# Last two output tiles of a diffusion trunk in parts of 384 and 128 tokens, the scale of the 128 by one product with ones

## The reference, cut to what matters

```python
def rmsnorm(x, g):
    xf = x.astype(jnp.float32)
    y = xf * lax.rsqrt(jnp.mean(xf * xf, axis=-1, keepdims=True) + EPS) * g.astype(jnp.float32)
    return y.astype(x.dtype)
...
    return (o * jax.nn.silu(z)) @ w_out          # ret_output
...
        x = x + gt_l[:, None, :] * ol
...
    return rmsnorm(x, final_g)
```

## Time and profile before

| | us |
|---|---|
| median of 3 runs | 953.13 |
| lowest and highest | 952.37, 954.92 |
| the profiled execution | 953.86 |
| its span, first to last instruction | 952.1 |
| TensorE busy in the span | 929.2 |
| VectorE, ScalarE, GpSimd busy | 556.5, 346.2, 243.7 |

### The profile page before, as it was taken

How to read it: one execution, slowest core, us unless ns; L and a number is a source line. 1 busy time by engine, 2 the same in 40 slices (tenths; PEclk the granted TensorE clock), 3 DMA queues, 4 the chain that set the end, 5 groups by cost and what they waited for, 6 DMA issues and landing times.

```text
span 952.1 us, 13121 instructions
## 1 busy us (share of the span) xinstructions
PE 929.2 (98%) x4852; PEld 804.2 (84%) x4852; DVE 556.5 (58%) x817; ACT 346.2 (36%) x587; POOL 243.7 (26%) x243
## 2 busy tenths in 40 slices
PE   5999999999999999999999999999999999999996
PEld 5989998888888888888888888888888888888886
DVE  6887769999985332358435545436435545468333
ACT  8443334323223332345323333324223333454222
POOL 4359840766554000014100321013100221011001
PEclk9999999999999999999999999999999999999998
DMA  9762233655545121212221122202211122102222
GB/s 353 290 222 86 92 111 112 202 180 193 185 168 225 64 67 67 89 45 89 67 67 45 45 70 86 66 1 88 66 66 44 44 66 66 56 10 89 92 85 88
DMA packets 28859, 98.71 MB, mean 104 GB/s; under 512 B 3816, under 2 KB 6024, under 8 KB 28560
## 3 DMA queue, kind: packets, MB, share of 16 engines
q1 hardware_dynamic: 26800, 91.04, 28.2%
q0 software_dynamic: 1744, 6.84, 1.9%
q10 hardware_dynamic: 272, 0.26, 0.1%
HBM read 96.01 MB, written 2.10 MB: 103 GB/s over the span
## 4 chain that ended last, share of the span: by engine, by line
PE 90%; DVE 4%; issue 2%; DMA 2%; POOL 1%; ACT 1%; SPq 0%; POOLq 0%; DVEq 0%
PE banks L1681 30%; PE banks L1682 29%; PE banks L1683 29%; DMA raw<-stream 1%; DVE wreg L1162 1%; DVE hreg L1431 0%; POOL gate L640 0%; DMA gate<-x_rows 0%; DVE gate L1153 0%; DVE gate L1156 0%; DVE hreg L1208 0%; PE banks L1952 0%; DVE dist L1172 0%; POOL gate L680 0%; PE banks L1825 0%
## 5 line engine op out<-in xcount | busy, mean ns | idle before, releaser
L1681 PE MATMUL banks<-hreg,ring 128*128 128x512 f32 (+2 forms) x940 | 334.0, 355 | 3.8 <-DVE hreg L1208 2.3
L1682 PE MATMUL banks<-hreg,ring 128*128 128x512 f32 (+2 forms) x940 | 332.1, 353 | 0.0
L1683 PE MATMUL banks<-hreg,ring 128*128 128x512 f32 (+2 forms) x940 | 330.0, 351 | 0.0
L1072 DVE TENSOR_TENSOR ring<-raw,ring 128x512 fp32r<-128x512 f32 x192 | 148.7, 790 | 231.8 <-ACT ring L692 230.5
L692 ACT ACTIVATE ring<-raw 128x512 fp32r<-128x512 f32 x192 | 118.9, 630 | 363.6 <-PE banks L1683 285.5
L1681 PEld LDWEIGHTS banks<-hreg,ring 128*128 128x128 f32 x940 | 177.8, 189 | 29.4 <-issue 3.6
L1683 PEld LDWEIGHTS banks<-hreg,ring 128*128 128x128 f32 x940 | 177.4, 189 | 22.2
L1682 PEld LDWEIGHTS banks<-hreg,ring 128*128 128x128 f32 x940 | 177.8, 189 | 21.7 <-issue 1.0
L607 POOL TENSOR_TENSOR gate<-xreg,gate 128x257 f32<-128x257 f32 (+1 forms) x64 | 72.3, 1160 | 75.5 <-ACT gate L834 58.0
L1104 DVE CUSTOM_DVE_ANT_0 dist<-raw,gate 128x1024 bf16<-128x1024 f32 x64 | 84.9, 1327 | 4.1 <-DMA raw<-stream 0.5
L640 POOL TENSOR_TENSOR gate<-gate 128x512 f32<-128x512 f32 x12 | 17.2, 1430 | 250.7 <-ACT gate L915 249.9
(11 more groups left out here) (224 smaller groups left out, 1099.6 us busy)
## 6 DMA issues: line engine op xcount, KB each, us to landing
raw<-stream SPq DMA_DIRECT2D x148, 512.0 KB, 3.3
gate<-stream SPq DMA_DIRECT2D x10, 512.0 KB, 11.0
gate<-x_rows SPq DMA_DIRECT2D x6, 512.0 KB, 6.9
gate<-x_lat POOLq DMA_DIRECT2D x1, 2048.0 KB, 8.7
xreg<-x_lat POOLq DMA_DIRECT2D x1, 2048.0 KB, 9.0
xreg<-stream SPq DMA_DIRECT2D x2, 512.0 KB, 12.5
gate<-cond_in SPq DMA_DIRECT2D x2, 512.0 KB, 9.1
gate<-x_ctx POOLq DMA_DIRECT2D x1, 1024.0 KB, 11.5
```

Source lines behind the costliest of these rows:

```text
L1072: dve.tensor_tensor(ring[:, n % 2, 1, c], raw[:, buf, c], f32(ring[:, n % 2, 0, c]), ALU.subtract).then_inc(split_done, 1)
L1681: pe.matmul(out, left[0], right[0], start=start, stop=False)
L1682: pe.matmul(out, left[0], right[1], start=False, stop=False)
L1683: return pe.matmul(out, left[1], right[0], start=False, stop=stop)
```

## The change

Tiles 6 and 7 are both made in two parts, the first of 384 tokens (`first`) and the second of 128 (`rest`), in the order: tile 6 first, tile 7 first, tile 7 rest, tile 6 rest. Since tile 6's weights are then used at the start and at the end, they are split into a place of their own, `w6` in `wreg` (columns 4096 to 8191), which is free by then; tile 7's weights go to `ring`. The loops over tiles 2 to 5 are written out on ScalarE and VectorE.

For the first 384 tokens the scale is made as before (three columns instead of two, one bank instead of two), inside the matmuls of the two `rest` parts: `sums_first` after kk 8 of tile 7 rest, `rows_first` after kk 1 of tile 6 rest. For the last 128 tokens the squares are the moving operand and the matrix of ones the weights (bank 5): this gives every partition the sum of each token at once. `sums_rest` adds acc_t and tile 7's squares after kk 10 of tile 6 rest; only tile 6's squares come after the last projection matmul. Square root and reciprocal then run on 128 columns, and no diagonal matrix and no second product are needed.

ScalarE multiplies all eight tiles by the final gain into tmp_t (`gain`), tiles 0 to 5 ahead of the parts. VectorE writes all outputs in instructions over two or four tiles (`scale_out`); GpSimd has no part in it any more. The stores are four of 2 tiles by 384 tokens and two of 4 tiles by 128 tokens, all on SyncE's queue.

```diff
@@ sync
+            first, rest = slice(0, FIRST), slice(FIRST, LAT)
+            for n, (c, a, b) in enumerate([(first, 2 * i, 2 * i + 2) for i in range(4)] +
+                                          [(rest, 4 * i, 4 * i + 4) for i in range(2)]):
+                sp.wait_ge(out_vec, n + 1)
+                sp.dma_start(out[a:b].rearrange("m p t -> p m t")[:, :, c],
+                             x3[:, a:b, c]).then_inc(s_out, 16)
@@ scalar
+            for n in (HOME1, HOME1 + 1):
+                buf, landed = raw_at("out1", n)
+                act.wait_ge(s_raw[buf], landed)
...
+                    act.activation(w6[0][:, n - HOME1, c], raw[:, buf, c], ACT.Copy).then_inc(hi_done, 1)
+            x2_sq(5, 1)
...
+            for m in range(6):
+                gain(m, slice(0, LAT))
...
+            def part_sq(n, m, c):
+                act.wait_ge(x2_part_done, n)
+                act.wait_ge(acc_done, m + (2 * KT + 4))
+                act.activation(sq_t[:, m % 2, c], x3[:, m, c], ACT.Square).then_inc(sq_part, 1)
+                gain(m, c)
+
+            part_sq(1, 6, first)
+            part_sq(2, 7, first)
+            act.wait_ge(sum_sq_done, 3)
+            act.activation(tok_rms[:, 0:3], bank(0, 3), ACT.Sqrt, scale=1.0 / D,
+                           bias=eps[:, :]).then_inc(end_root, 1)
+            part_sq(3, 7, rest)
+            part_sq(4, 6, rest)
+            act.wait_ge(sum_sq_done, 4)
+            act.activation(rstd_t[:, rest], bank(5, P), ACT.Sqrt, scale=1.0 / D,
+                           bias=eps[:, :]).then_inc(end_root, 1)
@@ vector
+            def scale_out(a, b, c, rstd):
+
+                n = b - a
+                dve.tensor_tensor(x3[:, a:b, c], tmp_t[:, a:b, c],
+                                  rstd.unsqueeze(1).to_broadcast([P, n, c.stop - c.start]),
+                                  ALU.mult).then_inc(out_vec, 1)
...
+            x2_part(3, 7, rest, bank(4, P))
+            dve.wait_ge(rows_spread, 1)
+            dve.wait_ge(gained, 6)
+            dve.wait_ge(x2_part_done, 2)
+            for m in (0, 2, 4):
+                scale_out(m, m + 2, first, bank(1, FIRST))
+            dve.wait_ge(gained, 8)
+            scale_out(6, 8, first, bank(1, FIRST))
+            x2_part(4, 6, rest, bank(3, P))
+            dve.wait_ge(end_root, 2)
+            link(dve.reciprocal(rstd_t[:, rest], rstd_t[:, rest]))
+            dve.wait_ge(gained, 10)
+            for m in (0, 4):
+                scale_out(m, m + 4, rest, rstd_t[:, rest])
@@ tensor
+            def last_part(m, c, o, between):
+
                 for kk in range(FT):
+                    if c is first and kk % 4 == 0:
+                        split(SLOT_OUT1 + 2 * m + kk // 8, kk // 4 % 2)
+                    if m == 6:
+                        w = tuple(w6[part][:, kk // 8, P * (kk % 8):P * (kk % 8) + P] for part in range(2))
+                    else:
+                        w = part_of(kk // 8, P * (kk % 8))
+                    last = mm3(o, w, (g1(kk, 0)[:, c], g1(kk, 1)[:, c]), kk == 0, kk == FT - 1)
+                    if kk in between:
+                        between[kk]()
+                last.then_inc(end_part, 1)
+
+            pe.wait_ge(x1_done, 6 + (2 * KT + 3))
+            last_part(6, first, bank(7, FIRST), {})
+            pe.wait_ge(x1_done, 7 + (2 * KT + 3))
+            last_part(7, first, bank(6, FIRST), {})
+            last_part(7, rest, bank(4, P), {8: sums_first})
+            last_part(6, rest, bank(3, P), {1: rows_first, 10: sums_rest})
+            pe.wait_ge(sq_part, 4)
+            pe.matmul(bank(5, P), ones[:, :], sq_t[:, 0, rest], start=False,
+                      stop=True).then_inc(sum_sq_done, 1)
```

More of the change, by code:

```diff
@@ L1670, in _, with x2_part @@
-            dve.wait_ge(x2_half, 2)
-            for m in (6, 7):
-                last_out(0, m)
-            token_rstd(1)
-            for m in range(POOL_TILES[1], KT):
-                last_out(1, m)
+            first, rest = slice(0, FIRST), slice(FIRST, LAT)
+            def x2_part(n, m, c, src):
+                dve.wait_ge(end_part, n)
+                dve.scalar_tensor_tensor(out=x3[:, m, c], in0=src, scalar=mod1[:, 24 + m, 0:1],
+                                         in1=x3[:, m, c], op0=ALU.mult,
+                                         op1=ALU.add).then_inc(x2_part_done, 1)
@@ L2070, in _ @@
-            pe.wait_ge(x2_half, 1)
-            for part in (acc_t, squares7):
-                if part is squares7:
-                    pe.wait_ge(sq_half, 2)
-                for b, i in ((6, 2), (7, 3)):
-                    last = pe.matmul(bank(b, 1), part[:, P * i:P * i + P], ones[:, 0:1],
-                                     start=part is acc_t, stop=part is squares7)
-            last.then_inc(sum_sq_done, 1)
-            token_rows(1)
+            for m in (4, 5):
+                pe.wait_ge(x1_done, m + (2 * KT + 3))
+                out_tile(SLOT_OUT1 + 2 * m, ((0, LAT, bank(7 - m % 2)),), g1)
@@ new lines, in _, with sums_first, rows_first @@
+            first, rest = slice(0, FIRST), slice(FIRST, LAT)
+            def sums_first():
+                pe.wait_ge(acc_part, 1)
+                pe.wait_ge(sq_part, 2)
+                for i in range(3):
+                    last = token_sum(bank(0, 1, i), i, (acc_t, sq_t[:, 1, :]))
+                last.then_inc(sum_sq_done, 1)
+            def rows_first():
+                pe.wait_ge(spread_done, 1)
+                for t in range(3):
+                    last = pe.matmul(bank(1)[:, P * t:P * t + P], ones[:, :], spread[:, t, :],
+                                     start=True, stop=True)
+                last.then_inc(rows_spread, 1)
@@ new lines, in sums_rest @@
+            def sums_rest():
+                pe.wait_ge(acc_done, 6 + (2 * KT + 5))
+                pe.matmul(bank(5, P), ones[:, :], acc_t[:, rest], start=True, stop=False)
+                pe.wait_ge(sq_part, 3)
+                pe.matmul(bank(5, P), ones[:, :], sq_t[:, 1, rest], start=False, stop=False)
+            def last_part(m, c, o, between):
+                for kk in range(FT):
+                    if c is first and kk % 4 == 0:
[8 more added lines that the diff above has]
+                last.then_inc(end_part, 1)
```

167 lines of the change are left out of this document (48 added, 119 removed).

## The result

| | us |
|---|---|
| kernel before, median of 5 runs | 953.13 (952.37 to 954.92) |
| changed kernel, median of 5 runs | 964.57 (962.11 to 964.79) |
| ratio, with its 95% interval | 1.011 (1.010 to 1.0121) |
| profiled execution of the changed kernel, its span | 962.11, 960.3 |

The change makes the kernel 1.1% slower, and 964.57 us lies outside the range that was forecast, 954.4 to 959.6.

The account below looks back on a forecast made before the run. TensorE, holding 90% of the chain of waits, was taken to bound the kernel. TensorE's +6.26 us and the tail's -3.65 us gave +2.6 us on 953.13, so 955.7 us, range 954.4 to 959.6.

Parts of the forecast that it names:

- TensorE's terms: TensorE up to its last projection matmul: 16.70 + 10.80 + 2.48 = 29.98 us against 23.72, 6.26 us later.
- The rival of overlapping weight loads: 128-column matmuls run at 0.081 us or 0.067 us each, giving 952.7 or 951.3 us, not slower; chance 0.06.
- the row: Profile row of 130-column matmuls, each with its own weight load: 0.113 us each; basis for 0.1125 us per 128-column matmul.
- The tail's terms: Chain behind the last projection matmul, residual to stores and end: 6.98 us against 10.63, 3.65 us saved.
- The store: Last store of 256 KB at the kernel's end: lands 2.5 us after issue, ends 2.3 and 3.4.
- The covers: Weight splits, ScalarE gains and VectorE's early outputs stay hidden behind TensorE; VectorE done 1.5 us before the last residual.
- The step that failed: In the 128-column parts the clock was taken to stay at full level; its fall was a rival, chance 0.2.
- the short stretch of 130 columns: Earlier stretch of 130-column matmuls at full clock, used as evidence against the clock falling in the 128-column parts.
- main case: All paces as the profile rows show: centre 955.7 us, from 954.8 to 957.0; chance 0.74.
- the long fall: All of tile 6 rest at half clock: 54 instructions x 0.11, 5.9 us more, 961.6 us; chance 0.08.
- that rival: The clock falls in the 128-column parts: 1.7 us more (957.4) or 5.9 us more (961.6); chance 0.2.

Follow-up runs that it names:

- e2: The changed kernel, with the six sums of the first 384 tokens streaming 128 columns of ones instead of one; 955.57 us, ratio 1.0036 to the kernel before.
- e6: The changed kernel, with the 128-token parts streaming 192 columns and using 128; 956.23 us, ratio 1.0034 to the kernel before.
- e9: The changed kernel, with VectorE adding tile 7's squares first, so 6 one-column instructions replace 12; 954.06 us, ratio 1.0017 to the kernel before.
- e1: The changed kernel, with the 128-token parts streaming 256 columns and using 128; 956.49 us, ratio 1.0048 to the kernel before.
- e4: The changed kernel, in the order tile 6 first, tile 6 rest, tile 7 first, tile 7 rest; 958.46 us, ratio 1.0064 to the kernel before.
- e5: The changed kernel measured again, unaltered; 962.7 us, ratio 1.0111 to the kernel before.
- e7: The kernel before, with the scale of tile 7's second half made by products with the matrix of ones; 954.0 us, ratio 1.0009.
- e10: Against the kernel before: tile 7 alone in 384 and 128 tokens (128 streamed as 192), GpSimd writing three output instructions; 954.34 us, ratio 1.001.

## Why the prediction was wrong

**TensorE's terms held as long as the clock did.** Both 384-column parts took 16.66 us (917.18 to 933.84; forecast 16.70). The 128-column pace was 0.1115 us and the 12 sums took 1.31 us to the next matmul (forecast 12 x 0.1125 = 1.35). The whole list, undisturbed, is e2's and e6's: 29.68 and 29.70 us against 23.60, so 6.1 us more where 6.26 was forecast.

**The rival of overlapping weight loads did not come.** Only the first matmul of a part followed after 0.06 us, as in the earlier trace rows; all others after 0.11. The Trainium skill, TensorE: Matmul & The Clock Gate, section Back-to-back issue gap, gives about 81 ns for such a stream; no stretch of matmuls of the last tiles shows it in any run here, and the row was the better guide.

**The tail's terms held too.** With the clock up, 7.30 us lie behind the start of the last matmul in e6, where before had 10.75: 3.45 us saved, forecast 3.65. The store landed after 2.5 us as taken. The covers held: VectorE was free 1.57 us before the last residual in e6, where 1.5 was forecast (6.16 in the slowed change), and TensorE did not stop.

Together, +2.65 us in e2 and e6 against the +2.6 forecast. That this is so close is in part luck: each of the two terms came out 0.2 us smaller, and the two errors cancel. Their ratios, 1.0036 and 1.0034, are some 0.7 us above that.

**The step that failed is the clock.** The argument "matmuls follow one another without a wait, and the short stretch of 130 columns kept 1.00" carried a main case of 0.74, and the long fall was left out of the range with a chance of 0.08. In the trace the matmuls do follow one another without a wait, TensorE is busy for 3.00 of every 3.00 us, and the clock falls. The price was sized about right: 54 instructions by 0.11, 5.9 us, 961.6; it was 56 instructions by 0.101 plus 0.44 in the tail, 6.1 us, and 962.11 for the profiled execution. (Tile 6 rest has 58 instructions, not 54: four of `sums_rest` were left out of the count.) The median, 964.57, is 2.5 us above that; see what stays open. Its chance was what was wrong.

What had been a clause in that rival, "in the middle the sums stream one column at a time", is one of two conditions. Taking away the one-column streaming (e2) or half of it (e9), or filling the 128-column matmuls to 192 or 256 (e6, e1), each keeps the clock at 1.00. Together with the 5.31 us of e4 without a fall: neither the thin matmuls nor the one-column products are enough alone, in this kernel at this place. The rows that the argument used were one with 8 thin matmuls and one with 12 short instructions among matmuls of 256 columns; neither has both, and I read them as if they spoke of the sum.

The trace of before had stronger evidence of both kinds, which the prediction left aside when it said that no stretch has such thin streaming for so long:

```profile
22.72 5.52 PE L1734 MATMUL banks<-csf,gate 128*128 128x128 f32 x48
24.00:28.00 4.00, 4.00 (x39) 4.00 (x38) 3.19 (x4) 1.13 (x1) 0.00 (x0) 1.00 1.03 416
411.35 1.89 PE L1916 MATMUL banks<-ones,gate 128*128 128x1 f32 x16
411.00:414.00 3.00, 3.00 (x28) 3.00 (x27) 0.40 (x2) 1.51 (x4) 0.00 (x0) 1.00 0.02 5
```

From 19.04 to 28.00 us TensorE issues 80 matmuls of 128 columns without a wait, and at 411.35 it issues 16 one-column instructions in a row between matmuls of 256 columns. The clock is at 1.00 in both. So each condition alone had been harmless at a size near the change's (96 thin matmuls, 12 one-column instructions), and the two together were seen nowhere.

The Trainium skill, same page, section HAM oscillation, blames waits between bursts for the falls of a thin-M kernel. By waits alone the packed stream would keep its clock; the measurement decides against it, since the stretch from 917.20 to the fall has no wait. It was used as an argument to lower the chance, and it should not have been.

**What stays open.** Three of the five runs of the change and one of the four of e5 took 2.2 to 2.8 us more than the others, with a mean granted clock of 0.985 or 0.986 instead of 0.987 to 0.989. They are part of why the change costs 10.5 us by the ratio and 8.8 by the traced stage. An estimate from the clock: 0.003 of 960 us is 2.9 us, so 5.8 us more at half level; that is 27 instructions at 0.2135 us, which cost 27 by 0.101, 2.7 us. That fits a fall 3 us earlier, at about 937.6, among the one-column sums. But no such execution was traced, and a low stretch elsewhere is not ruled out: in before, too, runs of 951.5 us have 0.997 and runs of 953.5 us 0.994, and what its trace has is half level from 56.6 to 60.0.

That low stretch shows another fall than this one: it began after TensorE had been idle for 2.25 us, behind eight matmuls of 130 columns, and the clock came back at 60.0 after 3.4 us of packed matmuls of 386 columns. Whether it would have come back near the end as well, had the matmuls grown dense again, isn't shown: in every fall of the last stage it stayed low to the end. And the runs show that both conditions together brought the fall, not why.

## What to carry to other kernels

Before cutting matmuls thinner to shorten a tail, look at what each stretch streams, and treat short products placed among thin matmuls as a risk to the clock even when TensorE never waits; the price is the number of instructions still to come times the difference between 0.2135 and 0.1125 us. Beside weight loads of 128 columns, up to 192 streamed columns were free here and can be streamed and thrown away to keep the clock. And where evidence about a cliff covers each of two conditions apart, the case that joins them belongs into the range.

## What the runs showed of the hardware that was not expected

- The granted clock fell from 1.00 to 0.50 with TensorE busy without a gap for more than 20 us (917.20 to 940.6), 2.5 us after 1.3 us of one-column matmuls inside a stretch of 128-column ones.
- At 0.50 the start-to-start time of a 128-column matmul with its own weight load went from 0.1115 to 0.2135 us, and the recorded weight load from 0.19 to 0.33 us. At full clock the columns do not set this pace (192 start as often as 128), and that was no shelter from the half level.
- Matmuls of 128 and of 192 columns both start every 0.11 us (e2, e6), those of 256 every 0.120.
- VectorE's outputs with all operands in SBUF were slower while GpSimd worked: in e7 0.99 and 0.94 us beside GpSimd and 0.47 behind its end, in e10 1.45 us beside and 0.68 behind. With the scales in PSUM, as in before, they took 0.47 us beside GpSimd, too.
